# Gates of expert blocks 64 to 127 by indirect accumulating transfers instead of one-hot products

## Chip, core and metric

The kernel runs on one NeuronCore of one Trainium2 chip. The metric is the device time of one execution in microseconds (us). The granted clock of TensorE is 1.000 of full speed over the whole profiled execution.

## What is computed

One decoder block for 256 tokens of width 1024: token mixers (attention), then a channel mixer with 16,384 experts. Only the channel mixer matters here. Each token picks 16 experts in each of 8 heads, with softmax weights g:

```python
e = i1 * PEER_NKEYS + i2                       # 128 x 128 experts, 8 heads x 16 picks a token
g = jax.nn.softmax(cv.astype(jnp.float32), axis=-1)
act = jax.nn.gelu(jnp.einsum('td,thkd->thk', xc, u[e]))
return jnp.einsum('thk,thkd->td', g * act, v[e])
```

## The kernel before

The channel mixer is computed densely. The experts lie in 128 blocks of 128 (block i1, row i2). U tile b (128 x 1024) times the normed tokens gives the activations of block b for all 256 tokens; they stay in SBUF in `big[:, b*T:(b+1)*T]`. Each is multiplied by its gate, a 128 x 256 matrix a block that is nearly all zeros, and V tile b is then multiplied by the weighted activations and summed in PSUM banks 0 to 3. float32 products are made of three fp32r products, of a high part (`hi`, `auxh`) and a low part (`lo`, `auxl`).

The order of work on each engine is written out by hand; semaphores join the engines.

- **SP** loads all tiles into the ring `raw` of four slots. `one` (L318 to L320) waits until `lo` of the tile four before is made (`lo_done`), and then issues the 512 KB load (L299).
- **ACT** makes `hi` of a tile (`loop_hi`, L1172) when the tile has landed and TensorE has used the tile three before it; `w_hi` (L1201) makes `auxh`.
- **DVE** makes `lo` (`loop_lo`, L1644).
- **GpSimd (POOL)** makes `auxl` (`w_lo`, L1904).
- **TensorE (PE)** does 24 matmuls of 256 columns a U tile (L803 to L805) and 12 of 512 columns a V tile (L862). The last two V tiles are done together (L877), and DVE adds the result (L1845).

The gates are made by one-hot products, four tokens at a time: ACT builds the one-hot of i2 (`squares_b`, `relu_b`: L1188, L1195), DVE that of i1 times the weight (`keys_equal` L1760, `rows_a` L1769), TensorE multiplies the two (`g_group`, L817, four matmuls of 128 columns), DVE adds high and low parts out of PSUM (`add_parts`, L1778) and multiplies into `big` (`weigh`, L1786). 64 groups beside U tiles 64 to 127 make the gates of blocks 0 to 63, and 64 more beside V tiles 0 to 63 make those of blocks 64 to 127. So one pass of V runs with groups, and one without.

The routing (top-16 choices, L1658 to L1745) is done on DVE and POOL beside U tiles 0 to 61. `router` is the end of it: weights in `gwt`, expert numbers in `i1f` and `i2f`.

Of the kernel before, what the change touches and what calls it, by code (L numbers as in the profile page):

```python
# [23 lines left out]
F32 = mybir.dt.float32  # L24
# [65 lines left out]
def build(nc, x_d, wpre_d, u_d, v_d, par_d, cst_d, kep_d, out_d):  # L90
    with ExitStack() as ctx:
        def sb(name, shape, dt=F32):
            return ctx.enter_context(nc.sbuf_tensor(name, shape, dt))

        def sem(name):
            return ctx.enter_context(nc.semaphore(name))
# [124 lines left out]
        rs2 = carve(2)  # L221
        assert at[0] <= NBLK * T

# [66 lines left out]
        def _(sp):  # L290
# [53 lines left out]
        def _(pe):  # L344
# [499 lines left out]
            each_tile(pe, NGRP, g_and_u)  # L844
            g_group(0, 0, NGRP)

# [46 lines left out]
        def _(act):  # L893
# [356 lines left out]
            squares_b(0, 1, NGRP)  # L1250
            relu_b(0, 1, NGRP)
            gelu_pair(0, HALF - 1, HALF)
            loop_hi(0, N_PRE + NBLK - 1 + SPLIT)


            def v_step_g(i, j):
                squares_b(i, j, NGRP + 2)
                w_hi(i, j + SPLIT - 1)
                relu_b(i, j, NGRP + 2)
                loop_hi(i, V0 + j + SPLIT)  # L1260

            def v_step(i, j):
                loop_hi(i, V0 + HALF + j + SPLIT)
                w_hi(i, HALF + j + SPLIT)

            each_tile(act, HALF - SPLIT, v_step_g)
            squares_b(0, HALF - 1, NGRP)
            w_hi(0, HALF - 1)
            relu_b(0, HALF - 1, NGRP)
            loop_hi(0, V0 + HALF)  # L1270
            loop_hi(0, V0 + HALF + 1)
            act.wait_ge(S("weighed"), 1 + NGRP + NGRP // 2)
            w_hi_tokens(HALF, 0, "whi_tokens")
            act.wait_ge(S("weighed"), 1 + 2 * NGRP)
            w_hi_tokens(HALF, 1, "whi_done")
            w_hi(0, HALF + 1)
            loop_hi(0, V0 + HALF + 2)
            w_hi(0, HALF + 2)
            each_tile(act, HALF - SPLIT, v_step)


        @block.vector
        def _(dve):
# [460 lines left out]
            link(dve.reciprocal(smx[:, 16:32], smx[:, 0:16]))  # L1744
            dve.tensor_tensor(g3, g3, smx[:, 16:32].unsqueeze(2).broadcast_to([P, 16, 16]), ALU.mult).then_inc(S("router"), 1)  # L1745
            dve.wait_ge(S("keysT"), 1)
# [82 lines left out]
            rows_a(0, 0, NGRP + 2)
            loop_lo(0, N_PRE + NBLK - 1 + SPLIT)  # L1830

            def v_step_g(i, j):
                group_step(i, j, NGRP + 1)
                loop_lo(i, V0 + j + SPLIT)

            each_tile(dve, NGRP - 4, v_step_g)
            for j in range(NGRP - 4, NGRP - 1):
                group_step(0, j, NGRP + 1, keys=False, rows=j == NGRP - 4)
                loop_lo(0, V0 + j + SPLIT)
            loop_lo(0, V0 + NGRP - 1 + SPLIT)  # L1840
            each_tile(dve, HALF - SPLIT, lambda i, j: loop_lo(i, V0 + HALF + j + SPLIT))
            dve.wait_ge(S("h_back"), 16 * TB)
# [6 lines left out]
        @block.gpsimd  # L1849
        def _(pool):  # L1850
            msb = cv_("msb").unsqueeze(1).broadcast_to([P, 2, 384])
            for p in range(4):

                if p:
                    pool.wait_ge(S("z_read"), p + 1)
                    pool.wait_ge(S("after"), p)
                    pool.tensor_tensor(stick_l, stick_x, msb, ALU.mult).then_inc(S("l_masked"), 1)

                pool.wait_ge(S("x_exp"), p + 1)
                if p:  # L1860
# [36 lines left out]

            V0 = N_PRE + NBLK

            def w_lo(i, b):  # L1900

                s = (V0 + b) % SPLIT
                pool.wait_ge(S("whi_done"), i * UNROLL + (b + 1))
                pool.tensor_tensor(auxl[:, s * T:(s + 1) * T], big[:, bass.ds(i * (UNROLL * T) + b * T, T)],  # L1904
                                   auxh[:, s * T:(s + 1) * T].bitcast(F32), ALU.subtract).then_inc(S("wlo_done"), 1)

            def w_lo_tokens(b, tb, ready, count, done):

                pool.wait_ge(S(ready), count)
                c0 = (V0 + b) % SPLIT * T + tb * P  # L1910
                pool.tensor_tensor(auxl[:, c0:c0 + P], big[:, b * T + tb * P:b * T + (tb + 1) * P],
                                   auxh[:, c0:c0 + P].bitcast(F32), ALU.subtract).then_inc(S(done), 1)

            def w_lo_behind_rows(i, j):
                pool.wait_ge(S("oneA_ready"), i * UNROLL + (NGRP + SPLIT + j + 1))
                w_lo(i, SPLIT + j)

            w_lo_tokens(0, 0, "whi_tokens", 1, "wlo_tokens")
            w_lo_tokens(0, 1, "whi_done", 1, "wlo_done")
            for b in range(1, SPLIT):  # L1920
                w_lo(0, b)
            each_tile(pool, HALF - SPLIT, w_lo_behind_rows)
            w_lo_tokens(HALF, 0, "whi_tokens", 2, "wlo_tokens")
            w_lo_tokens(HALF, 1, "whi_done", HALF + 1, "wlo_done")
            each_tile(pool, HALF - 1, lambda i, j: w_lo(i, HALF + 1 + j))

# [64 lines left out]
def constants():  # L1991
# [54 lines left out]
```

## Time and profile before

| | us |
|---|---|
| median of 3 runs | 1052.27 (1052.14 to 1052.61) |
| span of the profiled execution, first to last instruction | 1050.2 |
| what lies around the span (median less span) | 2.1 |
| PE / DVE / ACT / POOL busy | 1045.1 / 847.5 / 731.1 / 261.4 |
| V tiles with groups: PE time a tile | 3.19 |
| V tiles without groups: PE time a tile | 2.72 |

An engine's busy time says how full it is; what sets the end is the chain of work that ended last. The times of one tile in the table are differences of start times in that chain. "Idle before" of a row is the time in which its engine waited, with what released it.

### The profile page before, as it was taken

Reading aid. Unit: us, or ns where it says so; the run is one execution under the profiler, and the core shown is the slowest. Engines: PE = TensorE matmul, PEld = TensorE weight load, DVE = VectorE, ACT = ScalarE, POOL = GpSimd, SP = SyncE. Lnnn points to the kernel's source line nnn. Section 1 sums busy time; section 2 is a strip of 40 time slices with the busy share of each in tenths; the row PEclk is TensorE's granted clock in tenths of the full one; section 3 lists DMA queues with packets and bytes.
Section 4 is the critical chain, followed back from the end, with each engine's and each line's share of the span. In section 5 each row is a group of like instructions: output and inputs, shape, how many; then the busy total and the mean of one; then the engine's idle time right before and its main releaser. Section 6 shows DMA issues by size and latency. Waiting matters only on the chain.

```text
span 1050.2 us, 22234 instructions
## 1 busy us (share of the span) xinstructions
PE 1045.1 (100%) x7073; PEld 950.7 (91%) x7073; DVE 847.5 (81%) x1605; ACT 731.1 (70%) x1444; POOL 261.4 (25%) x213
## 2 busy tenths in 40 slices
PE   9999999999999999999999999999999999999998
PEld 7798899989999999999999999988888888888887
DVE  7768886788998889899999999999999995444444
ACT  5556776665544444599889888999999995454453
POOL 0000110017102127600000000134444444545543
PEclk9999999999999999999999999999999999999999
DMA  8643224564555555555444444455544465655553
GB/s 340 254 150 134 91 91 135 190 217 162 161 181 189 186 168 193 179 166 160 160 160 160 160 158 154 140 171 170 169 160 161 167 211 181 200 186 194 199 187 114
DMA packets 50305, 181.34 MB, mean 173 GB/s; under 512 B 5585, under 2 KB 5713, under 8 KB 50257
## 3 DMA queue, kind: packets, MB, share of 16 engines
q1 hardware_dynamic: 50112, 180.59, 51.6%
q8 instruction: 26, 0.43, 0.2%
q10 hardware_dynamic: 144, 0.14, 0.1%
q14 instruction: 23, 0.18, 0.0%
HBM read 178.62 MB, written 2.10 MB: 172 GB/s over the span
## 4 chain that ended last, share of the span: by engine, by line
PE 99%; DMA 0%; ACT 0%; DVE 0%; issue 0%; DVEq 0%
PE bank L862 33%; PE bank L803 12%; PE bank L805 12%; PE bank L804 12%; PE bank L817 5%; PE bank L357 2%; PE bank L358 2%; PE bank L359 2%; PE bank L423 2%; PE bank L743 2%; PE bank L427 1%; PE bank L439 1%; PE bank L440 1%; PE bank L441 1%; PE bank L720 1%; PE bank L721 1%
## 5 line engine op out<-in xcount | busy, mean ns | idle before, releaser
L1644 DVE TENSOR_TENSOR lo<-raw,hi 128x1024 fp32r<-128x1024 f32 x253 | 318.5, 1259 | 123.2 <-ACT hi L1172 122.9
L1172 ACT ACTIVATE hi<-raw 128x1024 fp32r<-128x1024 f32 x253 | 268.1, 1060 | 208.5 <-PE bank L805 113.3
L803 PE MATMUL bank<-xhi,hi 128*128 128x256 f32 x1024 | 292.8, 286 | 0.0
L805 PE MATMUL bank<-xhi,lo 128*128 128x256 f32 x1024 | 290.0, 283 | 0.0
L804 PE MATMUL bank<-xlo,hi 128*128 128x256 f32 x1024 | 289.7, 283 | 0.0
L1904 POOL TENSOR_TENSOR auxl<-big,auxh 128x256 fp32r<-128x256 f32 x126 | 167.7, 1331 | 198.9 <-ACT auxh L1201 198.9
L803 PEld LDWEIGHTS bank<-xhi,hi 128*128 128x128 f32 x1024 | 196.6, 192 | 0.0
L804 PEld LDWEIGHTS bank<-xlo,hi 128*128 128x128 f32 x1024 | 196.3, 192 | 0.0
L805 PEld LDWEIGHTS bank<-xhi,lo 128*128 128x128 f32 x1024 | 196.1, 191 | 0.0
L1188 ACT ACTIVATE oneB<-kep,eT 128x128 fp32r<-128x128 f32 x512 | 162.1, 389 | 0.0
L862 PE MATMUL bank<-hi,auxh 128*128 128x512 f32 x504 | 158.9, 396 | 0.0
L862 PE MATMUL bank<-lo,auxh 128*128 128x512 f32 x504 | 156.0, 391 | 0.0
L862 PE MATMUL bank<-hi,auxl 128*128 128x512 f32 x504 | 155.7, 390 | 0.0
L862 PEld LDWEIGHTS bank<-hi,auxl 128*128 128x128 f32 x504 | 94.6, 188 | 20.5
L862 PEld LDWEIGHTS bank<-lo,auxh 128*128 128x128 f32 x504 | 94.6, 188 | 20.0
L1294 DVE TENSOR_TENSOR lo<-raw,hi 128x1024 fp32r<-128x1024 f32 x73 | 90.1, 1244 | 27.2 <-ACT hi L906 26.9
L906 ACT ACTIVATE hi<-raw 128x1024 fp32r<-128x1024 f32 x73 | 77.1, 1058 | 48.0 <-PE bank L427 19.9
L862 PEld LDWEIGHTS bank<-hi,auxh 128*128 128x128 f32 x504 | 90.0, 189 | 15.1
L1778 DVE TENSOR_REDUCE gsum<-bank 128x256 f32<-128x512 f32 x128 | 88.0, 688 | 6.0 <-PE bank L817 1.2
L1769 DVE TENSOR_TENSOR oneA<-same,gw 128x512 fp32r<-128x512 f32 x128 | 87.8, 686 | 0.0
L1195 ACT ACTIVATE oneB<-oneB 128x512 fp32r<-128x512 f32 x128 | 79.0, 618 | 0.1
L817 PEld LDWEIGHTS bank<-oneA,oneB 128*128 128x128 f32 x512 | 72.2, 190 | 5.3 <-issue 0.4
(387 smaller groups left out, 1527.2 us busy)
## 6 DMA issues: line engine op xcount, KB each, us to landing
raw<-u_d SPq DMA_DIRECT2D x128, 512.0 KB, 3.3
raw<-v_d SPq DMA_DIRECT2D x128, 512.0 KB, 3.3
raw<-wpre_d SPq DMA_DIRECT2D x70, 512.0 KB, 4.2
big<-wpre_d SPq DMA_DIRECT2D x8, 512.0 KB, 8.5
big<-x_d SPq DMA_DIRECT2D x4, 256.0 KB, 3.9
out_d<-big SPq DMA_DIRECT2D x2, 512.0 KB, 5.8
big<-out_d SPq DMA_DIRECT2D x2, 512.0 KB, 5.2
out_d<-big SPq DMA_DIRECT2D x4, 256.0 KB, 2.0
```

What stands on the lines that cost most here:

```text
L803: pe.matmul(out, wh, xhi[:, k, :], start=(k == 0), stop=False)
L804: pe.matmul(out, wh, xlo[:, k, :], start=False, stop=False)
L805: m = pe.matmul(out, wl, xhi[:, k, :], start=False, stop=(k == KT - 1))
L817: m = pe.matmul(bank[6 + g % 2][:, 2 * t * HALF:2 * (t + 1) * HALF], oneB[:, g % 2, t, :], oneA[:, g % 2, t, :, :], start=True, stop=True)
L862: m = pe.matmul(bank[2 * b + f][:, :], a_, w_[:, s, f * 512:(f + 1) * 512], start=(first and st_ == 0), stop=False, skip_group_check=True)
L1172: act.activation(hi[:, slot(n), :], raw[:, splits(n) % RING, :], ACT.Copy).then_inc(hi_done, 1)
L1188: m = act.activation(oneB[:, g % 2, t, :], iota, ACT.Square, bias=i2, scale=-1.0)
L1294: dve.tensor_tensor(lo[:, slot(n), :], raw[:, splits(n) % RING, :], hi[:, slot(n), :].bitcast(F32), ALU.subtract).then_inc(lo_done, 1)
L1644: dve.tensor_tensor(lo[:, slot(n), :], raw[:, splits(n) % RING, :], hi[:, slot(n), :].bitcast(F32), ALU.subtract).then_inc(lo_done, 1)
L1769: dve.tensor_tensor(oneA[:, g % 2, :, :, :], eq_, w_.unsqueeze(3).broadcast_to([P, 4, 2, HALF]), ALU.mult).then_inc(S("oneA_ready"), 1)
L1778: dve.tensor_reduce(gsum[:, :, :], parts, AXX, ALU.add).then_inc(S("bank67_read"), 1)
L1904: pool.tensor_tensor(auxl[:, s * T:(s + 1) * T], big[:, bass.ds(i * (UNROLL * T) + b * T, T)], auxh[:, s * T:(s + 1) * T].bitcast(F32), AL ...
```

## The change

The 64 groups beside V are gone, with all their work on PE, ACT and DVE. Instead there is a DRAM tensor `gate_d` with one float for each (expert, token).

1. POOL clears blocks 64 to 127 of it with 16 transfers of 512 KB out of a zeroed tile `nought`: four before the first step of the stick-breaking attention, three after each of its four steps.
2. DVE works out addresses `chosen_at` behind the router (three instructions, at L1764 and L1766 of the new file), and keeps the weights in `chosen_w`.
3. POOL issues 256 indirect transfers. Each adds 128 weights, one a partition, at 128 addresses of `gate_d`. The 16 of one head and one half of the tokens go together; they wait until the 16 of the head before, same half, have landed.
4. SP waits for all of them behind the load of V tile 63 (and the two of `h`), then loads gate blocks of 128 KB into a ring `gring` of four slots.
5. DVE multiplies gate blocks into `big` (`gate_block`) and now also makes `auxl` (`w_lo`, till now on POOL).

```diff
@@ sync
-            stream(v_d, N_PRE + NBLK, HALF, HALF)
+            for b in range(TB):
+                sp.wait_ge(scattered[b], 16 * 16 * NH)
+            def v_and_gates(i, j):
+                sp.wait_ge(lo_done, i * UNROLL + splits(N_PRE + NBLK + HALF + j - RING + 1))
+                load(splits(N_PRE + NBLK + HALF + j) % RING,
+                     v_d[bass.ds(i * UNROLL + (HALF + j), 1)].rearrange("a p c -> (a p) c"))
+                sp.wait_ge(S("gated"), i * UNROLL + (j + 1))
+                sp.dma_start(gring[:, j % GRING, :], gate_tiles[bass.ds(i * UNROLL + (HALF + GRING + j), 1)].rearrange(
+                    "a p t -> (a p) t")).then_inc(gate_in[j % GRING], 16)
+            for m in range(GRING):
+                sp.dma_start(gring[:, m, :], gate_tiles[HALF + m]).then_inc(gate_in[m], 16)
+            each_tile(sp, HALF - GRING, v_and_gates)
+            for m in range(HALF - GRING, HALF):
+                sp.wait_ge(lo_done, splits(N_PRE + NBLK + HALF + m - RING + 1))
+                load(splits(N_PRE + NBLK + HALF + m) % RING, v_d[HALF + m])
@@ tensor
-            g_group(0, 0, NGRP)
-            each_tile(pe, NGRP - 1, g_and_v)
-            v_tile(0, 0, HALF, parts=2)
-            each_tile(pe, HALF - 3, lambda i, j: v_tile(i, j, HALF + 1))
+            each_tile(pe, NBLK - 3, lambda i, j: v_tile(i, j, 1))
@@ scalar
+            def w_hi_gated(i, m):
+                act.wait_ge(S("gated"), i * UNROLL + (m + 1))
+                w_hi(i, HALF + m)
+            def v_step_gated(i, j):
+                loop_hi(i, V0 + HALF + j + SPLIT)
+                w_hi_gated(i, j + SPLIT)
@@ vector
+            dve.wait_ge(S("cleared"), 16 * (HALF // 4))
+            link(dve.scalar_tensor_tensor(caf, i1f, 128.0, i2f, ALU.mult, ALU.add))
+            for b in range(TB):
+                m = dve.tensor_scalar(chosen_at[:, b * P:(b + 1) * P], caf[:, b * P:(b + 1) * P], float(T),
+                                      tok_at[:, b:b + 1], ALU.mult, ALU.add)
+            m.then_inc(S("chosen"), 1)
...
+            def gate_block(i, m):
+                dve.wait_ge(gate_in[m % GRING], i * (16 * (UNROLL // GRING)) + 16 * (m // GRING + 1))
+                of_block = big[:, bass.ds(i * (UNROLL * T) + (HALF + m) * T, T)]
+                dve.tensor_tensor(of_block, of_block, gring[:, m % GRING, :], ALU.mult).then_inc(S("gated"), 1)
...
+            gate_block(0, 0)
+            gate_block(0, 1)
+            w_lo(0, HALF - 1)
+            loop_lo(0, V0 + HALF)
+            loop_lo(0, V0 + HALF + 1)
+            gate_block(0, 2)
+            gate_block(0, 3)
...
+            def v_step_gated(i, j):
+                loop_lo(i, V0 + HALF + j + SPLIT)
+                gate_block(i, j + GRING)
+                w_lo(i, HALF + j + SPLIT)
+            each_tile(dve, HALF - GRING, v_step_gated)
@@ gpsimd
+            def clear(z):
+                pool.dma_start(gate_fours[HALF // 4 + z], nought.unsqueeze(1).broadcast_to([P, 4, T])).then_inc(S("cleared"), 16)
...
+            for h_ in range(NH):
+                for b in range(TB):
+                    if h_:
+                        pool.wait_ge(scattered[b], 16 * 16 * h_)
+                    for k in range(16):
+                        c = (b * NH + h_) * 16 + k
+                        pool.indirect_dma_start(gate_d, bass.IndirectOffsetOnAxis(chosen_at[:, c:c + 1], 0),
+                                                chosen_w[:, c:c + 1], None, compute_op=ALU.add).then_inc(scattered[b], 16)
```

SP's queue in the loop over V tiles 64 to 123, before (waits in brackets):

```order
L299 ISA [waits lo_done]
L299 DMA raw<-v_d 128x1024
L318 REGISTER_ALU
L299 ISA [waits lo_done]
L299 DMA raw<-v_d 128x1024
```

The same place of the change:

```order
L310 ISA [waits lo_done]
L310 DMA raw<-v_d 128x1024
L355 REGISTER_ALU
L356 ISA [waits gated]
L356 DMA gring<-gate_d 128x256
L352 REGISTER_ALU
L310 ISA [waits lo_done]
L310 DMA raw<-v_d 128x1024
```

Between one V load and the next there now stands a wait for `gated` (DVE's `gate_block`) and a gate load.

DVE at the start of that pass of the change and in its steps (before, each step there was one row, `lo<-raw,hi`):

```order
L1868 TENSOR_TENSOR big<-big,gring 128x256 [waits gate_in0,bank45_read]
L1868 TENSOR_TENSOR big<-big,gring 128x256 [waits gate_in1]
...
L1868 TENSOR_TENSOR big<-big,gring 128x256 [waits gate_in2]
L1868 TENSOR_TENSOR big<-big,gring 128x256 [waits gate_in3]
...
L1660 TENSOR_TENSOR lo<-raw,hi 128x1024 [waits hi_done]
L1868 ISA [waits gate_in1]
L1868 TENSOR_TENSOR big<-big,gring 128x256
L1853 REGISTER_ALU
L1854 TENSOR_TENSOR auxl<-big,auxh 128x256 [waits whi_done]
```

Each step makes `lo` of a V tile, weighs the block one further on, and makes `auxl` of the tile itself.

POOL behind the routing (`picked`), in the change:

```order
L1964 TENSOR_TENSOR big<-big 128x256 [waits placed] x32
L1975 DMA gate_d<-chosen_w,chosen_at 4194304x1 [waits router,chosen]
L1975 DMA gate_d<-chosen_w,chosen_at 4194304x1 x31
L1975 DMA gate_d<-chosen_w,chosen_at 4194304x1 [waits scattered0]
L1975 DMA gate_d<-chosen_w,chosen_at 4194304x1 x15
```

Where POOL made 126 rows `auxl<-big,auxh` beside V before, it now issues transfers only.

## Rows read from the trace of the kernel before

**Rows 1.** The page: busy times, and the chain that ended last

```profile
PE 1045.1 (100%) x7073; PEld 950.7 (91%) x7073; DVE 847.5 (81%) x1605; ACT 731.1 (70%) x1444; POOL 261.4 (25%) x213
...
PE 99%; DMA 0%; ACT 0%; DVE 0%; issue 0%; DVEq 0%
```

**Rows 2.** Stretches: window, length, busy us (instructions) by engine, clock, DMA share, GB/s

```profile
550.00:600.00 50.00, 50.00 (x424) 50.00 (x423) 46.66 (x76) 45.32 (x99) 0.00 (x0) 1.00 0.47 159
700.00:800.00 100.00, 100.00 (x504) 84.58 (x503) 97.22 (x158) 96.14 (x222) 43.45 (x32) 1.00 0.51 167
900.00:1000.00 100.00, 100.00 (x443) 82.81 (x442) 44.94 (x37) 50.56 (x74) 50.19 (x38) 1.00 0.58 192
```

**Rows 3.** Chain that ended last, in time: start us, us, what

```profile
668.73 2.80 PE bank L862 x12
...
697.72 2.80 PE bank L862 x12
...
819.06 2.80 PE bank L862 x12
...
870.16 171.44 PE bank L862 x756
1041.59 5.49 PE bank L877 x24
```

**Rows 4.** Timeline, 899 to 912 us, ACT, DVE and SP

```profile
900.19 1.06 ACT L1172 ACTIVATE hi<-raw 128x1024 fp32r<-128x1024 f32 x1 [1.35 <-PE bank L862]
902.91 1.06 ACT L1172 ACTIVATE hi<-raw 128x1024 fp32r<-128x1024 f32 x1 [1.35 <-PE bank L862]
901.28 1.23 DVE L1644 TENSOR_TENSOR lo<-raw,hi 128x1024 fp32r<-128x1024 f32 x1 [1.49 <-ACT hi L1172]
902.68 0.33 SPq L299 DMA_DIRECT2D raw<-v_d  x1
```

**Rows 5.** Tile raw, 900 to 950 us: loads of V

```profile
L299 SPq DMA_DIRECT2D raw<-v_d x19: 332/333/333, 900.0 to 948.9; - x19
...
DMA to landing us min/median/max: 3.1/3.2/3.5
```

**Rows 6.** Timeline of DVE, 460 us: `lo`, then instructions queued behind it

```profile
460.59 1.22 DVE L1644 TENSOR_TENSOR lo<-raw,hi 128x1024 fp32r<-128x1024 f32 x1
461.72 0.69 DVE L1778 TENSOR_REDUCE gsum<-bank 128x256 f32<-128x512 f32 x1
462.92 0.42 DVE L1786 TENSOR_TENSOR big<-gsum,big 128x256 f32 x1 [0.18 <-issue]
```

**Rows 7.** Timeline of SP, issues behind one another; chain: from a landing to ACT

```profile
15.30 0.33 SPq L299 DMA_DIRECT2D raw<-wpre_d  x1
15.67 0.91 SPq L313 DMA_DIRECT2D big<-wpre_d  x2
16.62 0.43 SPq L299 DMA_DIRECT2D raw<-wpre_d  x1
...
4.26 0.02 issue
4.28 0.96 ACT big L932 x3
```

**Rows 8.** Timeline of DVE and PE behind the router

```profile
449.18 0.42 DVE L1745 TENSOR_TENSOR big<-big 128x256 f32<-128x256 f32 x1
449.79 0.69 DVE L1747 COPY eT<-bank 128x512 f32<-128x512 f32 x1 [0.18 <-PE bank L830]
451.19 2.35 DVE L1644 TENSOR_TENSOR lo<-raw,hi 128x1024 fp32r<-128x1024 f32 x2
452.80 0.28 PE L803 MATMUL bank<-xhi,hi 128*128 128x256 f32 x1
```

**Rows 9.** Groups of DVE instructions by form: busy, mean ns

```profile
L1339 DVE SCALAR_TENSOR_TENSOR xlo<-bank,kep,xhi 128x256 fp32r<-128x256 f32 x8 | 3.2, 478 | 0.0
L1333 DVE TENSOR_SCALAR big<-kep,big 128x128 f32<-128x128 f32 x2 | 0.5, 283 | 0.0
```

**Rows 10.** POOL: timeline at 246 to 253 us, its group in 680 to 830 us, and DVE beside it at 439 us

```profile
250.44 0.74 POOL L1874 TENSOR_TENSOR big<-gw 128x256 f32<-128x256 f32 x1
251.14 1.72 POOL L1867 TENSOR_TENSOR xlo<-big,xhi 128x256 fp32r<-128x256 f32 x1
...
L1904 POOL TENSOR_TENSOR auxl<-big,auxh 128x256 fp32r<-128x256 f32 x48 | 62.9, 1311 | 88.3 <-ACT auxh L1201 88.3
...
438.92 1.73 DVE L1644 TENSOR_TENSOR lo<-raw,hi 128x1024 fp32r<-128x1024 f32 x1
```

**Rows 11.** Attention: timeline of POOL, and TensorE's first use of its product

```profile
110.06 1.55 POOL L1857 TENSOR_TENSOR big<-big 128x768 f32<-128x768 f32 x1 [5.54 <-DVE big L1529]
119.10 0.70 PE L647 MATMUL bank<-big 128*128 128x256 f32 x2
```

**Rows 12.** DMA queues, 0 to 60 us: packets, MB, share of 16 engines

```profile
q10 hardware_dynamic: 144, 0.14, 1.0%
```

More of the change, by code:

```diff
@@ L66 @@
 HALF = NBLK // 2
+GRING = 4
 EARLY = 7
@@ L117, in build @@
         oneB = sb("oneB", [P, 2, 4, P], F32R)
+        chosen_w = sb("chosen_w", [P, 2 * P])
+        chosen_at = sb("chosen_at", [P, 2 * P], U32)
+        gring = sb("gring", [P, GRING, T])
+        gate_d = nc.dram_tensor("gate_d", (NBLK * P * T, 1), F32, kind="Internal").ap()
+        gate_tiles = gate_d.rearrange("(e p t) o -> e p (t o)", e=NBLK, p=P)
+        gate_fours = gate_d.rearrange("(z e p t) o -> z p e (t o)", z=NBLK // 4, e=4, p=P)
         flatA, flatB = (oneA[:, :, :, :, :].rearrange("p q t r k -> p (q t r k)"),
@@ L159, in build @@
         g1 = kep[:, KEP["g1"][0]:KEP["g1"][0] + 8]
+        tok_at = kep[:, KEP["tok"][0]:KEP["tok"][0] + 2]
         xs = carve(TB * D).rearrange("p (b d) -> p b d", b=TB)
@@ L221, in build @@
         rs2 = carve(2)
-        assert at[0] <= NBLK * T
+        assert at[0] <= (NBLK - 1) * T
+        nought = carve(T, start=(NBLK - 1) * T)
         loaded = [sem(f"tile_loaded{i}") for i in range(RING)]
@@ L231, in build @@
         kep_in = sem("kep_in")
+        gate_in = [sem(f"gate_in{z}") for z in range(GRING)]
+        scattered = [sem(f"scattered{b}") for b in range(TB)]
         hi_done = sem("hi_done")
@@ L1249, in _, with v_step_weighed @@
                 w_hi(0, b)
-            squares_b(0, 1, NGRP)
-            relu_b(0, 1, NGRP)
             gelu_pair(0, HALF - 1, HALF)
             loop_hi(0, N_PRE + NBLK - 1 + SPLIT)
-            def v_step_g(i, j):
-                squares_b(i, j, NGRP + 2)
+            def v_step_weighed(i, j):
                 w_hi(i, j + SPLIT - 1)
-                relu_b(i, j, NGRP + 2)
                 loop_hi(i, V0 + j + SPLIT)
-            def v_step(i, j):
+            def w_hi_gated(i, m):
+                act.wait_ge(S("gated"), i * UNROLL + (m + 1))
+                w_hi(i, HALF + m)
+            def v_step_gated(i, j):
                 loop_hi(i, V0 + HALF + j + SPLIT)
-                w_hi(i, HALF + j + SPLIT)
-            each_tile(act, HALF - SPLIT, v_step_g)
-            squares_b(0, HALF - 1, NGRP)
+                w_hi_gated(i, j + SPLIT)
+            each_tile(act, HALF - SPLIT, v_step_weighed)
             w_hi(0, HALF - 1)
-            relu_b(0, HALF - 1, NGRP)
             loop_hi(0, V0 + HALF)
             loop_hi(0, V0 + HALF + 1)
[L1272 to L1276, printed above, removed]
+            w_hi_gated(0, 0)
+            w_hi_gated(0, 1)
             loop_hi(0, V0 + HALF + 2)
-            w_hi(0, HALF + 2)
-            each_tile(act, HALF - SPLIT, v_step)
+            w_hi_gated(0, 2)
+            each_tile(act, HALF - SPLIT, v_step_gated)
         @block.vector
@@ L1480, in _ @@
                 split_lo(n)
+            dve.wait_ge(tile_used, T_W1[7] + 1)
+            dve.memset(nought, 0.0).then_inc(S("nought"), 1)
             dve.wait_ge(S("sqk"), 3)
@@ L1744, in _ @@
             link(dve.reciprocal(smx[:, 16:32], smx[:, 0:16]))
-            dve.tensor_tensor(g3, g3, smx[:, 16:32].unsqueeze(2).broadcast_to([P, 16, 16]), ALU.mult).then_inc(S("router"), 1)
+            dve.tensor_tensor(chosen_w[:, :].rearrange("p (c k) -> p c k", k=16), g3,
+                              smx[:, 16:32].unsqueeze(2).broadcast_to([P, 16, 16]), ALU.mult).then_inc(S("router"), 1)
+            dve.wait_ge(S("cleared"), 16 * (HALF // 4))
[4 more added lines that the diff above has]
+            m.then_inc(S("chosen"), 1)
             dve.wait_ge(S("keysT"), 1)
@@ L1819, in _ @@
             for j in range(NGRP - 4, NGRP - 1):
-                u_step_g(0, j)
-            group_step(0, NGRP - 1, 0)
+                group_step(0, j, 0, keys=j + 3 < NGRP, rows=j + 2 < NGRP)
+                loop_lo(0, N_PRE + HALF + j + SPLIT)
+            group_step(0, NGRP - 1, 0, keys=False, rows=False)
             V0 = N_PRE + NBLK
-            add_parts(0, 0, NGRP)
-            keys_equal(0, 0, NGRP + 3)
-            dve.wait_ge(S("bank45_read"), NH + NBLK // 2)
-            weigh(0, 0, NGRP)
@@ L1829, in _, with w_lo @@
[L1829 to L1841, printed above, removed]
+            def w_lo(i, b):
+                s = (V0 + b) % SPLIT
+                dve.wait_ge(S("whi_done"), i * UNROLL + (b + 1))
+                dve.tensor_tensor(auxl[:, s * T:(s + 1) * T], big[:, bass.ds(i * (UNROLL * T) + b * T, T)],
+                                  auxh[:, s * T:(s + 1) * T].bitcast(F32), ALU.subtract).then_inc(S("wlo_done"), 1)
@@ new lines, in w_lo_tokens @@
+            def w_lo_tokens(b, tb, ready, count, done):
+                dve.wait_ge(S(ready), count)
+                c0 = (V0 + b) % SPLIT * T + tb * P
+                dve.tensor_tensor(auxl[:, c0:c0 + P], big[:, b * T + tb * P:b * T + (tb + 1) * P],
+                                  auxh[:, c0:c0 + P].bitcast(F32), ALU.subtract).then_inc(S(done), 1)
+            def gate_block(i, m):
+                dve.wait_ge(gate_in[m % GRING], i * (16 * (UNROLL // GRING)) + 16 * (m // GRING + 1))
+                of_block = big[:, bass.ds(i * (UNROLL * T) + (HALF + m) * T, T)]
+                dve.tensor_tensor(of_block, of_block, gring[:, m % GRING, :], ALU.mult).then_inc(S("gated"), 1)
@@ new lines, in _, with v_step_weighed @@
+            w_lo_tokens(0, 0, "whi_tokens", 1, "wlo_tokens")
+            w_lo_tokens(0, 1, "whi_done", 1, "wlo_done")
+            loop_lo(0, N_PRE + NBLK - 1 + SPLIT)
+            w_lo(0, 1)
+            def v_step_weighed(i, j):
+                w_lo(i, j + SPLIT - 1)
+                loop_lo(i, V0 + j + SPLIT)
+            each_tile(dve, HALF - SPLIT, v_step_weighed)
+            dve.wait_ge(S("bank45_read"), NH + NBLK // 2)
+            gate_block(0, 0)
+            gate_block(0, 1)
+            w_lo(0, HALF - 1)
@@ new lines, in _ @@
+            loop_lo(0, V0 + HALF)
+            loop_lo(0, V0 + HALF + 1)
+            gate_block(0, 2)
+            gate_block(0, 3)
+            w_lo(0, HALF)
+            w_lo(0, HALF + 1)
+            loop_lo(0, V0 + HALF + 2)
+            w_lo(0, HALF + 2)
+            def v_step_gated(i, j):
[3 more added lines that the diff above has]
+            each_tile(dve, HALF - GRING, v_step_gated)
+            loop_lo(0, V0 + NBLK - 1)
@@ L1842, in _ @@
+            w_lo(0, NBLK - 1)
             dve.wait_ge(S("h_back"), 16 * TB)
@@ L1850, in _ @@
         def _(pool):
+            def clear(z):
+                pool.dma_start(gate_fours[HALF // 4 + z], nought.unsqueeze(1).broadcast_to([P, 4, T])).then_inc(S("cleared"), 16)
+            pool.wait_ge(S("nought"), 1)
+            for z in range(4):
+                pool.wait_ge(lo_done, splits(T_KSB + 2 * z))
+                clear(z)
             msb = cv_("msb").unsqueeze(1).broadcast_to([P, 2, 384])
@@ L1862, in _ @@
                 pool.tensor_tensor(stick_a, stick_x, msb, ALU.mult).then_inc(S("a_ready"), 1)
+                for z in range(3):
+                    clear(4 + 3 * p + z)
             def xn_lo(k):
@@ L1896, in _ @@
                                        ALU.mult).then_inc(S("picked"), 1)
[L1898 to L1925, printed above, removed]
+            pool.wait_ge(S("chosen"), 1)
+            pool.wait_ge(S("router"), 1)
+            for h_ in range(NH):
[6 more added lines that the diff above has]
+                                                chosen_w[:, c:c + 1], None, compute_op=ALU.add).then_inc(scattered[b], 16)
     return nc
```

12 lines of the change are left out of this document (4 added, 8 removed).

## Prediction

> **What bounds the kernel now.** I read the page first. TensorE is busy for all of the span, and the chain that ended last is TensorE for 99% of it [rows 1]. So time is won only by taking instructions off TensorE, and lost only by making it wait. The stretches say where there is room beside it [rows 2]: U tiles with groups leave DVE 3.3 us of 50 idle and POOL all of them; V tiles with groups leave DVE 2.8 us of 100; V tiles without groups leave DVE 55 us of 100. The clock is 1.00 in all.
>
> The chain in order of time prices a V tile [rows 3]. With a group: (819.06 - 697.72) / 38 tiles = 3.193 us. Without: 171.44 / 63 tiles = 2.721 us. A group thus costs TensorE 0.472 us, more than its four matmuls' row would say, and 64 of them cost 30.2 us.
>
> **What the change removes.** V tile 0 started at about 668.5 us and 126 tiles lie before the last pair at 1041.59 [rows 3]. At 2.721 us each, and with the group ahead of tile 0 gone too, the pair would start at 668.1 + 126 x 2.721 = 1011.0. That is **-30.6 us**, if nothing makes TensorE wait.
>
> **V tiles 0 to 63.** DVE has `lo` (1.23) and `w_lo`. The second I price at 0.42, as the other product of two SBUF operands of 128 x 256 [rows 6]. Together 1.65 of 2.72: hidden. ACT loses the one-hots. Nothing is late here.
>
> **V tiles 64 to 127: a new loop.** This is the term I give most weight to. Before, a V load waited for `lo` of the tile four earlier. It was issued 0.17 us behind the end of `lo` (901.28 + 1.23, load at 902.68), landed 3.2 us later at 905.88, and its `hi` ran at 900.19 + 4 x 2.72 = 911.07 [rows 4, 5]: 5.2 us of slack.
>
> Now SP's order puts the wait for `gated` of block j, and a gate load, ahead of the V load of block j+1. DVE weighs block j in the step that makes `lo` of tile j-1. So the load of tile n waits for `lo` of tile n-2, and its landing releases `hi` and `lo` of tile n: a loop over two tiles. Its parts:
>
> - `hi` start to `lo` start: 901.28 - 900.19 = 1.09 [rows 4]
> - `lo` start to the next DVE instruction's start: 461.72 - 460.59 = 1.13 [rows 6]
> - `gate_block`: 0.42 [rows 6], DVE to SP: 0.17 [rows 4]
> - gate load's issue until the V load's: 0.45, between 15.67 - 15.30 = 0.37 and (16.62 - 15.67) / 2 = 0.48 [rows 7]
> - landing of the V load: 3.2 (3.1 to 3.5) [rows 5], and to start `hi`: 0.02 [rows 7]
>
> These add up to 6.48. The gate load's 128 KB goes ahead on the same engines but starts 0.45 earlier, so its share lies between nothing and 0.5 (8 packets an engine at 67 ns, that is 1.0% of 60 us x 16 over 144 packets [rows 12]); I take 0.12. The loop is **6.60 us for two tiles, where TensorE needs 5.44**: it is the bound, and the queue of SP is late, not the transfer rate (640 KB in 3.3 us is 200 GB/s, and 192 GB/s move today [rows 2]).
>
> How much it costs: the first late load is that of tile 65. Gate block 0 is weighed behind `lo` of tile 63; with `hi` of that tile at TensorE's start of tile 61, the load goes out 3.3 us later and lands at 6.5, where 5.44 was due: 1.1 us late. Every two tiles add 1.16, for 29 pairs until tile 123: 33.6. TensorE starts a tile 5.44 us behind a punctual `hi`, and `lo` is ready after 2.4, so it feels 3.0 less. The last four loads wait for no gates. **1.1 + 33.6 - 3.0 = +31.7 us.** Every 0.1 us of the loop is worth 2.9. With the loop at 6.38 (landing 3.1, no share) it is 25.4; with 6.9 (landing 3.5) 40.4.
>
> **The router.** Three DVE instructions go ahead of the copy into eT: 0.48 and 2 x 0.28 [rows 9], less some overlap, about 1.0 with the wait between them. The copy waited 0.18 for TensorE anyway, so `lo` at 451.19 starts 0.8 later and its first tile is ready at 453.2; TensorE needs it at 452.80 [rows 8]. **+0.4 us**, kept to the end.
>
> **The clears.** Three lie between POOL's two products of an attention step. POOL idles 5.5 us there, and TensorE first reads the product's result at 119.10, 7.5 us after its end [rows 11]. That is 13.0 us for three, 4.3 each. No row shows POOL issuing a transfer. From below, SP's 0.33 [rows 4]; from above, four times POOL's dearest 128 x 256 instruction, 1.72 [rows 10], since each clear writes four rows a partition: 6.9, which would cost three gaps 7.6 each, 23 us. I take the nearest single instruction, 1.55 [rows 11]: hidden, **0**.
>
> **The 256 indirect transfers.** They start at about 450.7 (449.6, the end of L1745 [rows 8], and 1.0). SP must see them landed by about 834: the first gate block is wanted on DVE behind `lo` of tile 63, at 668.4 + 61 x 2.721 + 2.3 = 836.7, and I allow 2.6 for its load (3.2 for four times the bytes). So each may cost POOL (834 - 450.7 - 3.2) / 256 = **1.48 us**. No row shows one. From below 0.33, SP's issue for as many rows [rows 4]. From above 1.72, an instruction of POOL that was caught behind one of DVE's; alone the like took 0.74 [rows 10]. Beside a DVE as busy as here it took 1.31 on average, and that is my value: 335 us, all landed at 789, 45 us early. **0.** The waits between heads lie 16 transfers back, over 20 us against a landing of 3.2, and cost nothing.
>
> The Trainium skill (SBUF — State Buffer, Who interferes with whom) speaks against that margin. It says that DVE and GpSimd share a pair of SBUF ports as an exclusive lock, and that a DVE instruction with two SBUF inputs keeps out a GpSimd instruction that reads SBUF. It also says that writing descriptors needs only the write side. By the first sentence an indirect transfer, which reads its addresses in SBUF, may pay the wait each time; by the second alone it would not. The 0.74 against 1.72 of [rows 10] agrees with the first for products. By the first the time would be rival B's 1114; by the second the sum below stays.
>
> **The sum.** -30.6 + 31.7 + 0.4 = +1.5. It is made on the profiled span of 1050.2, which lies 2.1 below the runs' median; on 1052.3 it gives **1053.8, say 1054**. Its own range is 1052.3 - 30.6 + 0.4 + 25.4 = 1047.5 to the same with 40.4, 1062.5. A measurement of this kernel tells about 0.2%, 2.1 us, from no change.
>
> **Rivals.**
>
> *A. The forecast: scatter hidden, the two-tile loop takes back the gain.* 0.62. For it: every part of the loop is a row. Of this, 0.14 is faster, 0.20 within 2.1 us, 0.28 slower.
>
> *B. The scatter is late.* POOL pays over 1.48 us for one. At 1.72 all lands at 894, 60 us late, and each us counts fully because SP's loads of V stand behind the wait: 1114. At 1.6, 1083. For it: the lock seen in [rows 10] and that DVE is 93 to 97% busy all through. Against: an address is one element a partition, not 256. 0.22.
>
> *C. The loop does not bind, and the gain stands.* This is the other side: 1052.3 - 30.6 + 0.4 = 1022. It needs a V load to land within 2.0 us of its issue, or SP to pass the wait for `gated` two steps earlier than I read. The break-even with today is a loop of 6.55. Against: 19 landings of 3.1 to 3.5 [rows 5]. 0.07.
>
> *D. POOL or the transfers slow U tiles 64 to 127.* An indirect transfer has 128 elements of 4 bytes. If each took an engine 67 ns [rows 12], 8 of them and a semaphore an engine 256 times are 154 us in 336, on top of the 0.47 share of the loads: near full. The loads have slack there, so it is hidden until twice that. Or DVE, with 0.22 us spare a tile, loses to POOL what it lost at 439 us, 1.73 against 1.23 [rows 10]: 0.5 for each of 2.5 transfers a tile, less the spare, is 1.0 us for 64 tiles, 64 us: 1118. I hold much less likelier, some 20 us with the dear clears: 1074. 0.09.
>
> **Range and chances.** From 1046, under A's low end, to 1096, which takes B up to 1.65 us a transfer. It leaves out C, the dearer part of B and of D, together just under 0.2. Faster 0.14 + 0.07 = 0.21; same 0.20; slower 0.28 + 0.22 + 0.09 = 0.59.
>
> **What the new profile would show.** V tiles 0 to 63 at 2.72 us each. V tiles 64 to 123 at 3.3 us, TensorE idle some 1.1 us in two tiles, ACT's `hi` waiting for the landing of `raw` rather than for TensorE, and V loads issued behind `gate_block`. POOL's transfers ending before 834. The forecast is wrong if ACT still waits for TensorE at V tiles 64 to 127 (C), if SP's loads of `gring` start later than 835 (B), or if U tiles with groups take more than today's 3.30 us (50 us over 424 / 28 tiles [rows 2]) (D).

## The result, and the profile after

| | us |
|---|---|
| before | 1052.2 (1051.93 to 1052.61) |
| after | 1253.96 (1253.56 to 1257.12) |
| ratio | 1.192 (95%: 1.191 to 1.194) |
| span of the profiled execution after | 1251.8 |

The change makes the kernel 201.8 us slower; 1054 was forecast, with 1046 to 1096 as the range.

The page of the changed kernel, against [rows 1]:

```profile
PE 1032.2 (82%) x6817; PEld 922.0 (74%) x6817; DVE 792.9 (63%) x1546; ACT 623.5 (50%) x1123; POOL 586.1 (47%) x355
...
PE   8999999999999999999999999980000048888887
...
PEclk9999999999999999999999999995555569999999
...
POOL 38%; PE 36%; issue 9%; DMA 9%; ACT 3%; DVE 2%; SPq 1%; DVEq 0%; POOLq 0%; ACTq 0%
POOL gate_d L1975 38%; DMA raw<-v_d 9%; PE bank L833 5%; PE bank L831 5%; PE bank L832 5%; ACT hi L1193 3%; PE bank L385 2%; PE bank L386 2%; PE bank L387 2%; PE bank L451 2%; PE bank L771 2%; PE bank L889 1%; DVE big L1868 1%; PE bank L455
...
L1975 POOL DMA_INDIRECT gate_d<-chosen_w,chosen_at x256 | 482.7, 1886 | 84.1 <-issue 77.7
```

TensorE has a hole of five slices in the middle (a slice is 31.3 us), and is only eight tenths busy behind it. The chain that ended last is no longer TensorE's: the indirect transfers (L1975) hold the largest part, and behind them comes the landing of V tiles. The last row has the price: 1.886 us busy for one on average, and 77.7 us of "issue" before 255 of them, 0.30 us each, in which POOL waited for nothing that the profile shows.

The stretches say where time went (columns: length, PE, PEld, DVE, ACT and POOL busy with their instructions, clock, DMA share, GB/s), against [rows 2]:

```profile
550.00:650.00 100.00, 100.00 (x846) 100.00 (x845) 93.28 (x151) 90.16 (x197) 86.28 (x46) 1.00 0.67 160
...
700.00:800.00 100.00, 100.00 (x442) 82.83 (x442) 57.58 (x74) 50.12 (x74) 88.72 (x38) 1.00 0.71 194
800.00:850.00 50.00, 40.98 (x181) 33.61 (x179) 21.66 (x28) 19.12 (x28) 43.91 (x21) 0.94 0.55 137
850.00:1010.00 160.00, 0.00 (x0) 0.00 (x0) 0.00 (x0) 0.00 (x0) 133.78 (x87) 0.50 0.23 0
1010.00:1050.00 40.00, 29.58 (x110) 23.11 (x111) 17.74 (x29) 12.33 (x18) 0.66 (x1) 0.81 0.55 173
...
1100.00:1150.00 50.00, 41.71 (x171) 31.05 (x171) 26.72 (x43) 19.12 (x28) 0.00 (x0) 1.00 0.58 185
```

U tiles 64 to 127 are as fast as before, with POOL busy beside them. V tiles 0 to 63 take 12 x 100 / 442 = 2.71 us each. Then TensorE stands still for all 160 us of a window in which POOL alone works, and behind that it is busy for 83 of 100. SP's waits name the reason (who waited for whom: us in total, times, longest):

```profile
SPq L348 <- DMA gate_d<-chosen_w,chosen_at: 183.5, 1, 183.5
```

SP's first gate load goes out at 1012.15, where the prediction had it due at 834.

**What one transfer costs.** POOL's row of time in three places of the changed kernel, with DVE's `lo` (L1660) beside it in the first two. First, U tiles with groups:

```profile
470.14 2.61 POOL L1975 DMA_INDIRECT gate_d<-chosen_w,chosen_at  x1 [0.30 <-issue]
473.05 1.56 POOL L1975 DMA_INDIRECT gate_d<-chosen_w,chosen_at  x1 [0.30 <-issue]
474.92 1.56 POOL L1975 DMA_INDIRECT gate_d<-chosen_w,chosen_at  x1 [0.30 <-issue]
...
470.09 1.23 DVE L1660 TENSOR_TENSOR lo<-raw,hi 128x1024 fp32r<-128x1024 f32 x1 [0.22 <-ACT hi L1193]
...
473.41 1.23 DVE L1660 TENSOR_TENSOR lo<-raw,hi 128x1024 fp32r<-128x1024 f32 x1 [0.22 <-ACT hi L1193]
```

Then V tiles 0 to 63, and the stretch in which DVE is idle:

```profile
703.63 2.42 POOL L1975 DMA_INDIRECT gate_d<-chosen_w,chosen_at  x1 [0.30 <-issue]
706.36 2.41 POOL L1975 DMA_INDIRECT gate_d<-chosen_w,chosen_at  x1 [0.30 <-issue]
...
703.39 1.23 DVE L1660 TENSOR_TENSOR lo<-raw,hi 128x1024 fp32r<-128x1024 f32 x1 [1.16 <-ACT hi L1193]
...
706.11 1.23 DVE L1660 TENSOR_TENSOR lo<-raw,hi 128x1024 fp32r<-128x1024 f32 x1 [1.16 <-ACT hi L1193]
...
899.27 1.56 POOL L1975 DMA_INDIRECT gate_d<-chosen_w,chosen_at  x1 [0.30 <-issue]
901.14 1.55 POOL L1975 DMA_INDIRECT gate_d<-chosen_w,chosen_at  x1 [0.31 <-issue]
```

Alone, one takes 1.56 + 0.30 = 1.86 us. In these rows one that starts inside `lo` takes longer by what `lo` still has to go, less 0.13 (470.09 + 1.23 - 470.14 = 1.18, and 1.05 more is paid; 703.39 + 1.23 - 703.63 = 0.99, and 0.86). One that starts 0.36 ahead of `lo` (473.05) pays nothing, though `lo` runs through most of it. In V tiles 0 to 63 the two lock together: 2.42 + 0.30 is just a tile's 2.72, so the next transfer starts inside the next `lo` again. On average it is (1009.1 - 450.2) / 255 = 2.19.

This agrees with the two statements of the Trainium skill (SBUF — State Buffer, Who interferes with whom) that the prediction weighed: a transfer's start, where it has addresses to read, waits for the DVE instruction with two SBUF inputs, and its later part runs on beside one. That the wait is for reading the addresses is the page's reason and not shown here; nor do these rows tell whether it needs the second input (the run one_input_ahead, below, asks that).

**The loop over V tiles 64 to 123**, at 1102 to 1108 in the changed kernel, SP, ACT and DVE:

```profile
1104.47 0.33 SPq L356 DMA_DIRECT2D gring<-gate_d  x1
1105.06 0.33 SPq L310 DMA_DIRECT2D raw<-v_d  x1
1106.95 0.33 SPq L356 DMA_DIRECT2D gring<-gate_d  x1
1107.54 0.33 SPq L310 DMA_DIRECT2D raw<-v_d  x1
...
1104.12 1.06 ACT L1193 ACTIVATE hi<-raw 128x1024 fp32r<-128x1024 f32 x1 [1.11 <-DMA raw<-v_d]
...
1105.21 1.23 DVE L1660 TENSOR_TENSOR lo<-raw,hi 128x1024 fp32r<-128x1024 f32 x1 [0.58 <-ACT hi L1193]
1106.35 0.42 DVE L1868 TENSOR_TENSOR big<-big,gring 128x256 f32 x1
```

It is the loop that the prediction drew: `hi` waits for the landing of `raw`; 1.09 later `lo`, 1.14 later the gate block, whose end sends the gate load, and behind it the V load. The chain in order of time has one V landing for each turn:

```profile
1043.08 3.28 DMA raw<-v_d
...
1229.84 4.43 DMA raw<-v_d
```

Between them lie 26 turns: 186.76 / 26 = **7.18 us for two tiles**, where 6.60 was forecast. The landings in the chain (from the issue of a load until its data is there) are 3.66 on average (3.08 to 4.76), against 3.1 to 3.5 in [rows 5].

### The profile page after: what moved, and what is told of

The parts are those of the page before. It is cut to its first block, busy times and chain, and to the rows that moved or that the text cites. A ratio compares the mean times of both kernels' runs of the same rounds, so it can differ in the third digit from the quotient of the medians.

```text
span 1251.8 us, 20979 instructions
## 1 busy us (share of the span) xinstructions
PE 1032.2 (82%) x6817; PEld 922.0 (74%) x6817; DVE 792.9 (63%) x1546; ACT 623.5 (50%) x1123; POOL 586.1 (47%) x355
## 4 chain that ended last, share of the span: by engine, by line
POOL 38%; PE 36%; issue 9%; DMA 9%; ACT 3%; DVE 2%; SPq 1%; DVEq 0%; POOLq 0%; ACTq 0%
POOL gate_d L1975 38%; DMA raw<-v_d 9%; PE bank L833 5%; PE bank L831 5%; PE bank L832 5%; ACT hi L1193 3%; PE bank L385 2%; PE bank L386 2%; PE bank L387 2%; PE bank L451 2%; PE bank L771 2%; PE bank L889 1%; DVE big L1868 1%; PE bank L455 1%; SPq L356 1%
## 5 line engine op out<-in xcount | busy, mean ns | idle before, releaser
L1975 POOL DMA_INDIRECT gate_d<-chosen_w,chosen_at x256 | 482.7, 1886 | 84.1 <-issue 77.7
L1660 DVE TENSOR_TENSOR lo<-raw,hi 128x1024 fp32r<-128x1024 f32 x253 | 318.7, 1260 | 211.3 <-ACT hi L1193 211.0
L889 PE MATMUL bank<-hi,auxh 128*128 128x512 f32 x504 | 163.2, 406 | 213.1 <-DVE auxl L1854 212.4
L831 PE MATMUL bank<-xhi,hi 128*128 128x256 f32 x1024 | 292.9, 286 | 0.2 <-DVE lo L1660 0.2
L1868 DVE TENSOR_TENSOR big<-big,gring 128x256 f32 (+1 forms) x64 | 26.6, 419 | 176.3 <-DMA gring<-gate_d 176.3
L1209 ACT ACTIVATE oneB<-kep,eT 128x128 fp32r<-128x128 f32 x256 | 81.1, 389 | 0.0
L1964 POOL TENSOR_TENSOR big<-big 128x256 f32<-128x256 f32 x32 | 40.6, 1288 | 39.7 <-DVE big L1746 39.7
L1956 POOL TENSOR_TENSOR big<-big 128x256 f32<-128x256 f32 x16 | 14.4, 924 | 90.6 <-DVE big L1679 75.0
L385 PE MATMUL bank<-xhi,hi 128*128 128x256 f32 x192 | 56.2, 293 | 0.0
```

Source lines behind the costliest of these rows:

```text
L385: pe.matmul(out, wh, xh, start=(k == 0), stop=False)
L831: pe.matmul(out, wh, xhi[:, k, :], start=(k == 0), stop=False)
L889: m = pe.matmul(bank[2 * b + f][:, :], a_, w_[:, s, f * 512:(f + 1) * 512], start=(first and st_ == 0), stop=False, skip_group_check=True)
L1209: m = act.activation(oneB[:, g % 2, t, :], iota, ACT.Square, bias=i2, scale=-1.0)
L1660: dve.tensor_tensor(lo[:, slot(n), :], raw[:, splits(n) % RING, :], hi[:, slot(n), :].bitcast(F32), ALU.subtract).then_inc(lo_done, 1)
L1964: pool.tensor_tensor(e3, e3, tki[:, at_:at_ + 16].unsqueeze(1).broadcast_to([P, 16, 16]), ALU.mult).then_inc(S("picked"), 1)
```

## Experiments

**no_transfers, no_transfers_ahead, half_ahead, ahead** ran together, with the kernel before at 1051.9.

no_transfers:

```diff
-            for b in range(TB):
-                sp.wait_ge(scattered[b], 16 * 16 * NH)
+            sp.wait_ge(S("chosen"), 1)
@@ gpsimd
-                        pool.indirect_dma_start(gate_d, ...)
```

> The 256 indirect transfers are left out, so the weights of blocks 64 to 127 stay zero; clears, addresses, gate loads and all of V are as in the change. Theory 1 (the two-tile loop of SP and DVE binds whenever gates are loaded beside V): 1052.3 - 30.6 + 0.4 = 1022, plus the loop. In the profile of the change the loop takes (1229.84 - 1049.87) / 25 = 7.20 us for two tiles, so 1.1 + 29 x 1.76 - 3.0 = 49 us: 1071. With the 6.60 us that the prediction gave the loop: 1054. Theory 2 (the loop is slow only as an aftermath of the late transfers, a cold TensorE and a ring that runs empty): 1022. POOL has nothing to do after the router in either.

Measured: **1079.4** (1076.1 to 1079.8). The loop binds with no transfer ever late. Theory 1 holds in kind and was 8 us short, because the loop is slower than in the change. It is 7.48 us here, from its V landings in the chain of waits, with 22 turns between the first row and the last:

```profile
863.45 4.41 DMA raw<-v_d
...
1028.09 3.27 DMA raw<-v_d
```

Its landings are 3.89 on average where the change has 3.66. Why they are longer without the transfers no run shows.

no_transfers_ahead moves the wait and the gate load behind the V load of three tiles later:

```diff
             def v_and_gates(i, j):
-                (load of V tile HALF + j)
+                v_load(i, j + AHEAD)          # AHEAD = 3
                 sp.wait_ge(S("gated"), i * UNROLL + (j + 1))
                 sp.dma_start(gring[:, j % GRING, :], ...)
```

> As no_transfers, and SP issues the V load three tiles earlier in its order than the wait for the weighed block and the gate load that stand ahead of it in the change; instructions, sizes and ring are the same. Theory 1 (the order of SP's queue makes the loop): V tiles at 2.72 us throughout and TensorE without idle time, 1022. Theory 2 (not the order but the added work binds: gate blocks and the low parts on DVE, or 128 KB more a tile in the DMA engines): 64 x 0.3 to 0.9 us more, 1040 to 1071.

Measured: **1023.8** (1023.7 to 1024.3), and nothing but SP's order differs from the run above: the order costs 55.6 us. In 850 to 1000 us of this run TensorE has no idle time, though 241 GB/s move, where the changed kernel's V tiles 64 on move 185:

```profile
850.00:1000.00 150.00, 150.00 (x663) 124.22 (x662) 104.68 (x167) 75.37 (x111) 0.00 (x0) 1.00 0.74 241
```

half_ahead issues the transfers `for h_ in range(4)`, half of them.

> SP's order as in no_transfers_ahead, and the transfers of heads 0 to 3 alone, 128 of them; the weights of heads 4 to 7 of blocks 64 to 127 are left out. Theory 1 (a transfer costs POOL 2.2 us beside DVE and nothing else pays for it until SP waits): the 128 are landed at about 450 + 128 x 2.21 = 733 + 3, 100 us before SP wants them, and the time is that of no_transfers_ahead within 2 us. Theory 2 (rival D, POOL's transfers take something from DVE or from the loads of U): 5 us or more above no_transfers_ahead, with U tiles over 3.32 us.

Measured: **1023.65** (1023.6 to 1024.6), the same. 128 transfers are free: U tiles keep the pace of [rows 2] (424 matmuls in 50 us), and nothing is paid until SP waits.

ahead is the whole change with the new order.

> The whole change with SP's order of no_transfers_ahead: all 256 transfers. Theory 1 (lateness and loop are two separate costs that add): SP's loads of gates start at 1012, 178 us after the 834 at which they were due, so no_transfers_ahead + 178 + some 4 us for a TensorE that starts cold: about 1204, 50 us under the change. Theory 2 (the loop is part of the same wait): within 10 us of the change, 1244 to 1264.

Measured: **1204.3** (1201.8 to 1205.0). Late transfers cost 1204.3 - 1023.8 = 180.5, and the loop 1254.0 - 1204.3 = 49.7 on top: two separate costs. The 180.5 is 178.2 from 834 to 1012.2 and about 2.6 for two tiles behind the hole. TensorE had stood idle for 174 us, done one tile and waited 4 us more; its granted clock is 0.50 (1.2 GHz) from 1024 to 1028 and 1.00 (2.4 GHz) from 1029 on. These are 24 matmuls in the changed kernel's chain:

```profile
1023.91 8.01 PE bank L889 x24
```

against 2 x 2.72 at full clock.

**six_heads_ahead**, 192 transfers (`for h_ in range(6)`). This and the next three ran together, the kernel before at 1052.0.

> As the run ahead, with the transfers of heads 0 to 5 alone, 192 of 256; the weights of heads 6 and 7 of blocks 64 to 127 are left out. Theory 1 (only the count of transfers times their price decides when SP goes on): in the run ahead some 166 of them were issued when TensorE ran dry at 841, and each later one takes 1.86 us, so 192 are landed at 841 + 26 x 1.86 + 3 = 893, 59 us after the 834 at which SP wants them: 1023.8 + 59 + 3 for the cold start = 1086. Theory 2 (the wait for the other half's head, or something fixed, makes the lateness): more than 15 us away from that.

Measured: **1084.5** (1083.1 to 1087.3). The time follows the count: 128 free, 192 cost 60.7, 256 cost 180.5.

**half_rows_ahead**: `chosen_at[0:64, c:c + 1]`, `chosen_w[0:64, c:c + 1]`.

> As the run ahead, all 256 transfers, but each of 64 partitions rather than 128; half of the weights of blocks 64 to 127 are left out. Theory 1 (the 1.56 us that a transfer takes POOL alone is written descriptor by descriptor): about 0.8 to 0.9 us each beside an idle DVE, and all are landed before 834, so 1024. Theory 2 (it is fixed for an instruction): 1.56 us each again and 1204.

Measured: **1159.9** (1159.4 to 1160.5), between the two and nearer to theory 2. POOL's row, beside U tiles:

```profile
601.07 1.41 POOL L1978 DMA_INDIRECT gate_d<-chosen_w,chosen_at  x1 [0.30 <-issue]
602.79 1.42 POOL L1978 DMA_INDIRECT gate_d<-chosen_w,chosen_at  x1 [0.31 <-issue]
```

64 rows fewer save 0.15 of 1.56: the price is nearly all for the instruction. My 0.8 to 0.9 was wrong.

**plain_ahead**: `compute_op=ALU.add` left out.

> As the run ahead, but the transfers write rather than add. Theory 1 (adding costs the DMA engines, not POOL): 1.56 us each beside an idle DVE and 1204 us. Theory 2 (adding makes POOL's part dearer): under 1.4 us each and less than 1165.

Measured: **1031.8** (1031.1 to 1032.5): theory 2.

```profile
599.87 1.75 POOL L1978 DMA_INDIRECT gate_d<-chosen_w,chosen_at  x1 [0.30 <-issue]
601.92 0.97 POOL L1978 DMA_INDIRECT gate_d<-chosen_w,chosen_at  x1 [0.30 <-issue]
```

Writing takes POOL 0.97 where adding takes 1.56, and the last of 256 is issued at 837.6, so that only some 8 us are lost. The DMA queue of these transfers holds 976 packets for 31 of them in 50 us, where adding ones in the changed kernel had 2628 for 19 in 40 us: 31 against 138 packets each. The packets are not POOL's price either: the adding transfers of half_rows_ahead made 2164 for 28, 77 each, and took 1.41. It is no version to use, since a token may pick one expert in two heads, and then the weights must be summed.

**no_transfers_small_gates**: `gring[:, j % GRING, 0:32]` from the fifth block on, an eighth of each gate block; the rest is left out.

> As no_transfers (SP's order as in the change, no indirect transfers), with gate loads of 32 columns from the fifth block on: 16 KB rather than 128 KB. It separates the two terms of the loop that the prediction undersized. Theory 1 (the 128 KB ahead of the V load in the same DMA engines make its landing 3.6 rather than 3.2 us): landings near 3.2, a loop near 6.8 us, 1079.4 - 29 x 0.4 = 1067. Theory 2 (the landings are long because two V loads of a pair overlap, and the gate load costs next to nothing): within 3 us of 1079.

Measured: **1064.2** (1063.8 to 1064.7). The V landings in the chain, 23 turns:

```profile
860.82 3.20 DMA raw<-v_d
...
1018.35 3.36 DMA raw<-v_d
```

The loop is 157.53 / 23 = 6.85, the landing 3.34 on average against 3.89 in no_transfers: gate loads of 128 KB rather than 16 KB cost the V load 0.55, not the 0.12 of the prediction. The run makes all gate loads small. So it doesn't separate the one 0.59 ahead of the V load from the next, which in no_transfers goes out (905.34) while the V load of 902.70 is still under way.

**one_input_ahead** and **tokens_split** ran together (the kernel before at 1052.3).

```diff
-                dve.tensor_tensor(lo[...], raw[...], hi[...].bitcast(F32), ALU.subtract)
+                dve.tensor_scalar(lo[...], raw[...], 0.0, None, ALU.mult)
```

> As the run ahead, with all 256 adding transfers, but DVE makes lo of every tile in the loops by an instruction with one SBUF input (raw times 0) rather than two, so the low parts of U and V are left out. In the trace of the change a transfer that starts while lo runs takes as much longer as lo still has to go (2.42 and 2.61 us against 1.56). Theory 1 (only an instruction with two SBUF inputs holds up a transfer's start): most transfers of V tiles 0 to 63 take 1.56 us, two every 3.72 us rather than one every 2.72, all are landed by about 940 and the time is some 65 us under that of ahead, 1140. Theory 2 (any DVE instruction on SBUF of that length does): transfers of over 2 us stay, and the time is within 20 us of 1204.

Measured: **1138.5** (1138.45 to 1138.56), theory 1's time, but not by its mechanism. In V tiles 0 to 63:

```profile
703.16 1.93 POOL L1977 DMA_INDIRECT gate_d<-chosen_w,chosen_at  x1 [0.30 <-issue]
...
707.26 1.89 POOL L1977 DMA_INDIRECT gate_d<-chosen_w,chosen_at  x1 [0.30 <-issue]
709.46 1.56 POOL L1977 DMA_INDIRECT gate_d<-chosen_w,chosen_at  x1 [0.30 <-issue]
...
704.31 0.69 DVE L1663 TENSOR_SCALAR lo<-raw 128x1024 fp32r<-128x1024 f32 x1 [1.69 <-ACT hi L1196]
```

The instruction with one input takes 0.69 rather than 1.23, and in these rows a transfer that starts inside one still pays. They come every 2.72 from 704.31, so one runs from 707.03 to 707.72: at 707.26 it has 0.46 to go, and 0.33 is paid, less by the same 0.13 as beside `lo` with two inputs. The transfer at 703.16 pays 0.37 though it starts 1.15 ahead of one. So DVE's part in the price is shown (256 transfers are done 63 us sooner), and a second input is not what it takes: this instruction has one.

The Trainium skill (SBUF — State Buffer, Who interferes with whom) has `tensor_scalar` among the operations that can enter a mode with both port pairs and then hold GpSimd up; 0.69 against 1.23, with 0.33 and 0.37 still paid, agrees.

**tokens_split** takes what was free: 128 transfers, for tokens 0 to 127, and one-hot groups for tokens 128 to 255, 32 beside V tiles 0 to 31. POOL makes `w_lo` again.

```diff
+            for n in range(FIRST):            # FIRST = 84
+                add_weights(n)                # one transfer, tokens 0 to 127
...
+            for b in range(SPLIT, HALF):
+                if b - SPLIT < NG2 - SPLIT:   # NG2 = 32
+                    pool.wait_ge(S("oneA_ready"), NGRP + b + 1)
+                w_lo(0, b)
+                if n < 16 * NH:
+                    add_weights(n)
+                    n += 1
```

> A version within what was measured: the gates of blocks 64 to 127 come by 128 transfers for tokens 0 to 127 and by 32 one-hot groups beside V tiles 0 to 31 for tokens 128 to 255. POOL issues 84 transfers first, then one behind each low part that it makes again as in the kernel before; SP's order as in the run ahead; gate loads and weighing of 128 tokens. The whole is computed. Theory 1 (transfers are free while they are landed by 834 or so, a group costs TensorE 0.47 us): 1023.8 + 32 x 0.472 = 1039, that is 0.987 of the kernel before. Theory 2 (POOL can't make low parts and issue adding transfers in one V tile, 1.3 + 0.3 + 2.4 us against 3.19): TensorE waits for the low parts, 20 to 40 us more, no better than the kernel before.

Measured: **1042.05** (1041.5 to 1043.6), 0.991 of the kernel before (0.989 to 0.992). 3 us above theory 1. From 758 to 811 the chain in order of time goes through POOL: a low part and a transfer follow one another there, also where no group stretches a tile:

```profile
761.72 1.34 POOL auxl L1987
763.05 0.15 issue
763.21 3.16 DMA gate_d<-chosen_w,chosen_at
...
798.36 1.85 POOL auxl L1987
800.21 0.17 issue
800.37 1.56 POOL gate_d L1980
801.93 1.21 POOL auxl L1987
```

**tokens_split_2**: `FIRST = 88`, and `if n < 16 * NH and (b < NG2 or b % 2)`.

> As tokens_split, with 88 rather than 84 transfers ahead of POOL's low parts, and from V tile 32 on, where no group stretches a tile to 3.19 us, one transfer every second tile rather than every tile. In tokens_split the chain of waits goes through POOL from 755 to 807: a low part of 1.0 to 1.85 and a transfer of 1.56, with their gaps, take 2.72 us and more, and one wait of 3.16 for a landing stands among them. Theory 1 (those 50 us cost the 3 us by which it missed 1039): 1039 to 1040.5. Theory 2 (the 3 us lie elsewhere, with the clears, the router or the start of the gates): 1042 again.

Measured: **1038.4** (1038.2 to 1040.0), theory 1 and a little under its range; **0.987** of the kernel before (0.985 to 0.989): the fastest version that computes the whole.

## Why the prediction was wrong

**The step that failed: "The 256 indirect transfers", at 1.31 us each and hidden.** A transfer costs POOL 2.19 us from start to start. Of that 0.97 is writing 128 rows alone, 0.59 is for adding (both by plain_ahead), 0.30 is the gap at issue, and 0.33 is DVE. The break price of 1.48 was right in kind: at 2.19 all are landed at 1012, 178 us late, and each of these us counted. The forecast missed its size in three ways. I took 1.31 from a product of 128 x 256 that DVE held up [rows 10], as if an address list must be cheaper, though the run with half the rows shows the rows hardly matter. I gave POOL no gap between instructions. And I held 1.72 for an upper bound because it was POOL's dearest single instruction of that size; nothing made it a bound for another kind of instruction. Rival B named the mechanism with 0.22, and its dearest price was also too low: by its own line 1.72 gives 1114. The rest adds up: 1053.8, 178.2 for lateness, 18.0 for the loop above its forecast, 2.6 at the lower clock and 1.7 for low parts (below) are 1254.3, against 1254.0.

Even alone, at 1.86, 256 transfers need 476 us of the 383 to be had. DVE made it worse and did not decide it.

**The two-tile loop, +31.7.** Right in mechanism and place, undersized: 55.6 without transfers and 49.7 in the change. Its parts in the change: landing 3.66 for 3.32, gate load to V load 0.59 for 0.45, landing to `hi` 0.10 for 0.02; 7.18 for 6.60. By the prediction's formula 1.1 + 29 x 1.74 - 3.0 = 48.6. The largest of them is the landing. The prediction bracketed the gate load's share between nothing and 0.5 and then took 0.12; no_transfers_small_gates has 0.55 for it. The dear end of its range took a landing of 3.5 with that 0.12. With its own 0.5 the loop would have been 7.28 and the term 51.5, and the measured one would have been inside.

**TensorE without the groups, -30.6; router, +0.4; clears, 0.** These gave 1022, and no_transfers_ahead has 1023.8. POOL's first product stands at 110.06 in both kernels, so the clears are hidden; a clear takes 0.77 (0.75 to 0.98), and 1.55 was allowed. TensorE's wait at the router is 0.2 us. It waits 1.7 us more in three places for the low parts that DVE now makes (L1856 and L1863 of that run), which the prediction called hidden.

**Rival C** (the loop doesn't bind) fell with no_transfers. **Rival D** fell with half_ahead. U tiles keep their pace, DVE's `lo` takes 1.23 there as before, and U's loads land in 3.3 (3.2 before). It is DVE that holds up POOL. The transfers' packets took 17% of the DMA engines' time in 600 to 640 us of the change, where D's sum had 154 of 336 us.

## What to carry to other kernels

A hidden queue of equal small instructions is free up to a count and costs its full length beyond it: work out that count, and don't cover an unseen instruction's price with the duration of another kind; where it is unseen, take the gap between instructions into it too, and let the range reach well beyond the guess (here the price was 1.7 times it). Where the count doesn't fit, split the work by what one instruction covers (here tokens), and leave the rest in the old way. In a queue that issues in order, put a wait for late work behind the loads that need not wait for it: that was worth 50 us here with the same instructions.

## What was not expected of the hardware

- An adding indirect transfer of 128 single floats took POOL 1.56 us and one that only writes 0.97; with 64 floats, adding, 1.41. The adding ones made 138 packets each in the DMA queue, the others 31.
- Every indirect transfer stood 0.30 us behind the one before on POOL (255 gaps, 77.7 us).
- A transfer of 2.42 us and a tile of 2.72 us locked in step: from 681.87 to 836.92 each transfer beside V tiles started inside DVE's next `lo`. With half the rows the price stayed 2.42 there, though alone it was 1.41.
- A direct transfer of 512 KB from POOL took 0.77 us to issue, half of an indirect one of 512 bytes.
